# Gate columns of the delta rule as TensorE's weights, and its output in two groups of matmuls

## What is computed

```python
beta = jax.nn.sigmoid(dn_b)                       # dn_b, dn_a: 4 + 4 columns of the projection h @ w_in
g = -jnp.exp(dn_A_log) * jax.nn.softplus(dn_a + dn_dt_bias)

def step(state, inp):                             # over 4 chunks of 64 tokens, for 4 heads
    u_c, w_c, a_c, qd_c, kt_c, dl_c = inp
    v_new = u_c - jnp.einsum('bhck,bhkv->bhcv', w_c, state)
    o = jnp.einsum('bhck,bhkv->bhcv', qd_c, state) + jnp.einsum('bhcj,bhjv->bhcv', a_c, v_new)
    state = state * dl_c[..., None, None] + jnp.einsum('bhck,bhcv->bhkv', kt_c, v_new)
    return state, o
```

## Time and profile before

| | |
|---|---|
| median of 3 runs | 1917.99 us (1915.57 to 1919.57) |
| the profiled execution's own time | 1917.77 us |
| its span | 1916.0 us |
| mean granted clock of TensorE | 0.993 |
| TensorE matmul, busy | 1888.3 us (99%), 14788 records |
| VectorE, busy | 1252.2 us (65%) |
| ScalarE, busy | 956.3 us (50%) |
| GpSimd, busy | 308.2 us (16%) |

### The profile page before, as it was taken

The page is one execution under the profiler, slowest core; times in us unless marked ns, Lnnn a source line. Parts: engine busy times, 40 slices in busy tenths (PEclk is TensorE's granted clock), DMA queues, the critical chain, the costliest instruction groups (busy, mean ns, idle before and its releaser), DMA issues.

```text
span 1916.0 us, 35058 instructions
## 1 busy us (share of the span) xinstructions
PE 1888.3 (99%) x14788; PEld 1806.2 (94%) x14788; DVE 1252.2 (65%) x1678; ACT 956.3 (50%) x1381; POOL 308.2 (16%) x176
## 2 busy tenths in 40 slices
PE   7999999999999999999999999999999999999998
PEld 7999998998899999999989999999999899999998
DVE  6884567665689545777648775576647694567643
ACT  5634456444563345564445445555534445556533
POOL 0050221000003103200001352320001352221000
PEclk9999999999999999999999999999999999999999
DMA  6443344666545323555565553456655663445553
GB/s 227 160 143 111 112 154 153 205 195 209 163 135 165 111 99 122 201 173 190 193 195 176 183 187 122 133 181 190 191 187 171 218 193 115 136 169 187 186 188 100
DMA packets 92156, 317.50 MB, mean 166 GB/s; under 512 B 11744, under 2 KB 12896, under 8 KB 91744
## 3 DMA queue, kind: packets, MB, share of 16 engines
q1 hardware_dynamic: 91424, 314.69, 50.2%
q10 hardware_dynamic: 576, 0.57, 0.1%
HBM read 304.99 MB, written 1.05 MB: 160 GB/s over the span
## 4 chain that ended last, share of the span: by engine, by line
PE 84%; DVE 11%; ACT 2%; DMA 1%; issue 1%; SPq 0%; DVEq 0%; ACTq 0%
PE bank L2001 82%; DVE wlo L1126 4%; DVE area L1126 3%; DVE area L1132 1%; DMA raw<-in_weights 1%; ACT area L630 1%; PE bank L2512 1%; DVE hl L1132 1%; DVE xT L1132 1%; ACT whi L636 1%; PE bank L2220 1%; DVE area L1645 1%; DVE area L1643 0%; PE bank L2530 0%; ACT L618 0%
## 5 line engine op out<-in xcount | busy, mean ns | idle before, releaser
L1126 DVE TENSOR_TENSOR wlo<-raw,whi 128x1024 fp32r<-128x1024 f32 x518 | 666.3, 1301 | 402.6 <-ACT whi L636 402.2
L2001 PE MATMUL bank<-hh,whi 128*128 128x256 f32 x2928 | 834.5, 286 | 15.1 <-DVE wlo L1126 11.7
L2001 PE MATMUL bank<-hh,wlo 128*128 128x256 f32 x2928 | 818.2, 280 | 0.0
L2001 PE MATMUL bank<-hl,whi 128*128 128x256 f32 x2928 | 811.3, 280 | 0.0
L636 ACT CAST whi<-raw 128x1024 fp32r<-128x1024 f32 x572 | 589.4, 1046 | 415.7 <-PE bank L2001 369.9
L2001 PEld LDWEIGHTS bank<-hh,whi 128*128 128x128 f32 x2928 | 555.7, 190 | 28.4 <-DVE wlo L1126 15.1
L2001 PEld LDWEIGHTS bank<-hl,whi 128*128 128x128 f32 x2928 | 555.2, 191 | 1.9 <-issue 1.9
L2001 PEld LDWEIGHTS bank<-hh,wlo 128*128 128x128 f32 x2928 | 556.0, 190 | 0.0
L1781 POOL TENSOR_TENSOR area<-area 128x512 f32<-128x512 f32 (+4 forms) x86 | 136.7, 1596 | 567.8 <-DVE area L1132 249.8
L1781 POOL TENSOR_TENSOR wlo<-raw,whi 128x1024 fp32r<-128x1024 f32 x54 | 134.3, 2488 | 427.9 <-ACT whi L636 427.9
L2001 PE MATMUL bank<-area 128*128 128x128 f32 (+5 forms) x1544 | 199.9, 288 | 1.2 <-DVE area L1196 0.7
(11 more groups left out here) (127 smaller groups left out, 1918.3 us busy)
## 6 DMA issues: line engine op xcount, KB each, us to landing
raw<-in_weights SPq DMA_DIRECT2D x572, 512.0 KB, 4.1
area<-area SPq DMA_DIRECT2D x96, 64.0 KB, 3.6
area<-area SPq DMA_DIRECT2D x16, 128.0 KB, 4.0
cst<-in_const SPq DMA_DIRECT2D x1, 1188.0 KB, 8.3
cst<-in_const SPq DMA_DIRECT2D x1, 1024.5 KB, 6.9
xT<-in_x SPq DMA_DIRECT2D x4, 256.0 KB, 8.1
out<-xT SPq DMA_DIRECT2D x4, 256.0 KB, 2.9
area<-in_lev SPq DMA_DIRECT2D x2, 384.0 KB, 6.6
```

The source lines that it names most:

```text
L1126: return v.tensor_tensor(dst, x, y, op)
L2001: return e.matmul(ps, x, y, start=start, stop=stop, skip_group_check=skip)
```

## The change

The gate columns: SW becomes TensorE's weights (16 or 8 columns) and the 256 tokens move, in 16 matmuls which stand before chunk 4. They give a tile of 16 rows (8 of the high part and the small products, 8 of the low part) by 256 tokens. DVE copies it to `ABR` in SBUF inside the hook. After chunk 4 two matmuls with a constant of two stacked 8 x 8 unit matrices, sent along with `small`, transpose it and add the two parts, and DVE multiplies by RST straight from the bank. ACT's cast to SW and DVE's subtraction move one step ahead. The output: for n > 0 first four matmuls with the state's weights, then four with VN, and only the first matmul into each bank sets the start flag.

```diff
-N_SMALL = 64 + 512
+N_SMALL = 64 + 512 + 8
...
+        ABR = SM[0:16, 0:256]
...
                 def hook():
                     factor(norm)
-                    a.wait_ge(s_small[L], 16)
-                    a.copy(SW[:, :, 0:8], sm3).then_inc(*a_dn.up("SW", L))
...
                 next(qkv)
                 next(qkv)
+                a.wait_ge(s_small[L], 16)
+                a.copy(SW[:, :, 0:8], sm3).then_inc(*a_dn.up("SW", L))
                 next(qkv)
                 next(qkv)
                 a.wait_ge(*v_dn.at("ab", L))
...
                 def hook():
                     factor(norm)
-                    v.wait_ge(*a_dn.at("SW", L))
-                    tt(SW[:, :, 8:16], sm3, SW[:, :, 0:8].bitcast(F32), OP.subtract).then_inc(*v_dn.up("SW", L))
+                    v.wait_ge(*e_dn.at("abrow", L))
+                    v.tensor_copy(ABR, bank[1][0:16, 0:256]).then_inc(*v_dn.up("abrow", L))
...
                 next(qkv)
                 next(qkv)
+                v.wait_ge(*a_dn.at("SW", L))
+                tt(SW[:, :, 8:16], sm3, SW[:, :, 0:8].bitcast(F32), OP.subtract).then_inc(*v_dn.up("SW", L))
                 next(qkv)
                 next(qkv)
-                two = bank[1][:, 0:32].rearrange("p (s c) -> p s c", s=2)
                 v.wait_ge(*e_dn.at("ab", L))
-                v.tensor_copy(tmp2, two[:, :, 8:16]).then_inc(*v_dn.up())
-                v.wait_ge(*v_dn.now())
-                tt(AB2, two[:, :, 0:8], tmp2, OP.add).then_inc(*v_dn.up("absum", L))
-                v.wait_ge(*v_dn.now())
                 v.wait_ge(*v_norm.at("turned", norm))
-                tt(AB2, AB2, wide(RST[:, :], 2, 8), OP.mult).then_inc(*v_dn.up("ab", L))
+                tt(AB2, bank[1][:, 256:272].rearrange("p (s c) -> p s c", s=2), wide(RST[:, :], 2, 8), OP.mult).then_inc(*v_dn.up("ab", L))
...
+                    def place(h):
+                        return bank[2 + h // 2][:, 256 * (h % 2) + 64 * n:256 * (h % 2) + 64 * n + 64]
+
+                    if n:
+                        for h in range(4):
+                            mm(place(h), St[:, 128 * h:128 * h + 128], Aq[:, 256 * h + 64 * n:256 * h + 64 * n + 64], h % 2 == 0, False, True)
                     for h in range(4):
                         b = 2 * h + half
-                        o = bank[2 + h // 2][:, 256 * (h % 2) + 64 * n:256 * (h % 2) + 64 * n + 64]
-                        if n:
-                            mm(o, St[:, 128 * h:128 * h + 128], Aq[:, 256 * h + 64 * n:256 * h + 64 * n + 64], True, False)
-                        x = mm(o, hv(VN)[r, h, :], AT[r, 128 * b + 64 * q:128 * b + 64 * q + 64], n == 0, True)
+                        x = mm(place(h), hv(VN)[r, h, :], AT[r, 128 * b + 64 * q:128 * b + 64 * q + 64], n == 0, True, True)
...
                 next(qkv)
                 next(qkv)
                 next(qkv)
+                e.wait_ge(*v_dn.at("SW", L))
+                fresh(1, v_dn.at("ab", L))
+                for k in range(8):
+                    mm(bank[1][0:16, 0:T], SW[:, k, :], hh[:, k, :], k == 0, False, True)
+                    x = mm(bank[1][0:8, 0:T], SW[:, k, 0:8], hl[:, k, :], False, k == 7, True)
+                x.then_inc(*e_dn.up("abrow", L))
                 next(qkv)
-                e.wait_ge(*v_dn.at("SW", L))
-                fresh(1, v_dn.at("absum", L))
+                e.wait_ge(*v_dn.at("abrow", L))
                 for s in range(2):
-                    for k in range(8):
-                        mm(bank[1][:, 16 * s:16 * s + 16], hh[:, k, 128 * s:128 * s + 128], SW[:, k, :], k == 0, False, True)
-                        x = mm(bank[1][:, 16 * s:16 * s + 8], hl[:, k, 128 * s:128 * s + 128], SW[:, k, 0:8], False, k == 7, True)
+                    x = mm(bank[1][:, T + 8 * s:T + 8 * s + 8], ABR[:, 128 * s:128 * s + 128], small[0:16, 576:584], True, True)
                 x.then_inc(*e_dn.up("ab", L))
...
+        small[l][0:16, 576:584] = np.tile(np.eye(8, dtype=np.float32), (2, 1))
```

More of the change, by code:

```diff
@@ L398, in program @@
         u1, u2 = SM[:, 128:136], SM[:, 144:152]
-        AB2, tmp2 = (SM[:, c:c + 16].rearrange("p (s c) -> p s c", s=2) for c in (192, 224))
+        AB2 = SM[:, 192:208].rearrange("p (s c) -> p s c", s=2)
         AB = SM[:, 192:208].rearrange("p (s c) -> p c s", s=2)
+        ABR = SM[0:16, 0:256]
         sm3 = small[:, 0:64].rearrange("p (k c) -> p k c", c=8)
```

## The result

| | before | after |
|---|---|---|
| median | 1915.57 us (1910.08 to 1919.57, 5 runs) | 1926.87 us (1925.66 to 1929.29, 5 runs) |
| ratio | | 1.0064, 95% interval 1.0047 to 1.0081 |
| span of the profiled execution | 1916.0 us | 1925.1 us |

A forecast was written before the change was run, and what follows sets the result against it. The prediction took TensorE (PE), busy 99% of the span, to bound the kernel. Gate columns 3.0, output 5.3 and clock 3.4 us sum to 11.7 us off 1917.8, so 1906.1 us, range 1900.5 to 1912.5.

The forecast's parts named there:

- rival 5: DVE stands in the hook for the 16 new matmuls: time level at 0.47 us each, 1932.5 at half clock; chance 0.03.
- The gate columns, 3.0 us: Cheaper gate-column matmuls; chunk 13 gains only what DVE's row gains: 1.0 us in layer 0, 2.0 in layer 1.
- Rival 1: Gate columns give all of PE's saving, 2 x 4.3 us, DVE's row being tighter or ACT earlier: 1900.5 us; chance 0.08.
- the sign of being wrong that the prediction names: Chunk 13 starting much sooner than 55.4 (layer 0) or 553.1 less layer 0's gains (layer 1) would show the forecast wrong.
- The output, 5.3 us: Delta rule's output: grouping four St, then four VN saves array-shape changes, 0.89 us in each of six groups.
- rival 4: Grouping the delta rule's output saves only the VN half, about 0.5 us each, 3 us: 1908.3 us; chance 0.05.
- the upper bound of a group: Delta rule's output: at most 1.05 us saved per group (6.3 in all), if St costs what VN does.
- The clock, 3.4 us: After the output groups of layers 0 and 1, both falls of the clock to half vanish, saving 3.4 us.
- rival 3: The clock has nothing to do with the change, all four falls stay: 7.1 us off, 1910.7 us; chance 0.08.
- Rival 2: The clock still falls twice after the outputs, or at other places: 3.4 us less saved, 1909.4 us; chance 0.17.
- The sum, 11.7 us: Whole kernel: 3.0 + 5.3 + 3.4 us off 1917.8 us, giving 1906.1; chance 0.57 for its own range 1904 to 1909.

The follow-up runs named there:

- experiment 1: The kernel before with only 8 unused columns added behind `small`, moving every tile behind it 32 bytes: 1941.22 us, ratio 1.0157.
- 3: The kernel before with only the delta rule's output grouped, all addresses as before: 1905.64 us, ratio 0.9951.
- 8: The kernel before with 16 more columns of `small`, everything behind it 64 bytes further on: 1948.54 us, ratio 1.0179.
- 4: The changed kernel's gate columns alone, output in pairs as before, tiles 64 bytes higher: 1946.83 us, ratio 1.0185 to the kernel before.
- experiment 9: The changed kernel with hh, hl, RSB, SW and the area 128 bytes behind their old place: 1919.68 us, ratio 1.0035 to the kernel before.
- experiment 5: The changed kernel with RST moved behind the area, so hh, hl, RSB, SW and the area keep their old addresses: 1902.85 us, ratio 0.9919 to the kernel before.
- 6: The changed kernel with hh, hl and RSB 32 bytes on, the area at its old place: 1916.15 us, ratio 1.0012 to the kernel before.
- 7: The changed kernel with the area 32 bytes on, hh, hl, RSB and SW at their old places: 1905.23 us, ratio 0.9962 to the kernel before.
- 12: The changed kernel with hh, hl, RSB, SW and the area 256 bytes behind their old place: 1904.74 us, ratio 0.9944 to the kernel before.

## Why the prediction was wrong

**The step that failed is one that was never made.** The sum costs what the diff removes, adds and moves among the instructions. Its first line, `N_SMALL = 64 + 512 + 8`, stands in no term: the place of the tiles behind it was put at nothing, without a reason. It moves the operands of nearly every matmul by 32 bytes, and that costs 29 us (experiment 1), two and a half times everything forecast. The prediction also took 0.11 to 0.12 us as *the* distance of a 256-column matmul and never asked why it varies by 4% within one trace, from 113 to 118 ns. No rival has it either: rival 5, the one on the slower side, was DVE standing in the hook for the 16 matmuls, and these took 1.98 us in all.

**What bounds the kernel** was right, and it is why the move costs so much: PE is busy 99% of the span, so 27.3 us more of matmul time make 29 us.

**The gate columns, 3.0 us.** Right within 0.4 us in this pair of traces: from the norm's sum to chunk 13 layer 0 gained 1.2 us (forecast 1.0), and in layer 1 the kernel went from 2.40 us behind to 0.25, 2.15 (forecast 2.0). The other traces bear it out. Where the gate columns are new, from the norm's sum to chunk 13 is 30.8 us in both layers of all ten. Where they are old, it is 32.05 and 32.98 (before), 32.69 and 31.98 (experiment 1), 30.93 and 31.39 (3), 32.96 and 32.31 (8). That is 3.4, 3.1, 0.7 and 3.7 us for both layers together, 2.7 on average, and the least where the clock fell for the shortest time. Rival 1 is refuted by it. What is missing to its 4.3 us per layer is, as argued, lost to waits for wlo such as the one before chunk 13, 0.38 us before 53.95. Chunk 13 at 53.95 instead of 55.4 looked like the sign of being wrong that the prediction names; nearly all of it is the 1.3 us of the start.

**The output, 5.3 us.** The group of n = 2 is 0.84 us shorter, 0.89 was forecast, and rival 4 with its 0.5 us is refuted by that. The runs give 6.6 us at the old place and 9.9 at 64 bytes for the term and its share of the clock (forecast: 5.3 and up to 3.4, so 8.7). Two slips of the working carry no weight: 0.84 is 58% of 1.45 us and not half, and the upper bound of a group is 1.03 us and not 1.05.

**The clock, 3.4 us.** Right in kind: experiments 3 and 4 each remove the falls of one place. By the records of the clock in all fourteen traces, it fell at the old gate columns in both layers of all four traces that have them, and at the new ones in none of twenty cases. It fell in or within a microsecond behind 12 of 24 output groups in pairs, and behind 2 of 60 grouped ones (the one at 681.4 us in the changed kernel and one in experiment 9). So rival 3, that the clock has nothing to do with the change, is refuted, and with it the reading that only idle gaps of PE matter: PE was busy throughout in all those stretches. Rival 2 was half right: where the clock falls and for how long, 3.4 or 6.8 us, changes from one trace to the next, and one fall is left in the changed kernel. The Trainium skill (TensorE: Matmul & The Clock Gate, "HAM oscillation") warns of gaps in which PE is idle, but does not say that nothing else makes the clock fall. The prediction read that into it, and the falls here are a case that the section does not cover.

**The sum, 11.7 us.** At a fixed place it was of the right size: 14.35 us at 32 bytes, 11.6 at 64, and 10.8 by the medians at the old place (0.81% by the ratio, which is 15.5 us, with an interval of 0.48% to 1.14%). The first two are differences of times from different comparisons, in which the kernel before had other medians; by the ratios to it they are 0.9% and 0.4%, 18 and 8.5 us. So the size is known to within several us only, and these times can't tell rivals 1 and 4 from the forecast, as the rows above do. The forecast of 1906.1 us is thus the time of a kernel that was not the one changed: experiment 5 took 1902.85. That it came so near is in part luck, for the kernel before took 1912 to 1916 us in the comparisons and not the 1917.8 that the sum starts from.

## What to carry to other kernels

Read a diff for what it moves in memory as well as for what it moves in time: a table that grows, a new tile or another order of allocation shifts every operand behind it, and in a kernel bound by TensorE, as this one is, that can outweigh the change. Before a change is judged, print the addresses of both versions and hold those of the matmuls' operands fixed, or time the old kernel at the new addresses too; one look at the distance of matmuls in code that the diff does not touch tells whether this is needed. And where a mean distance is made of two kinds of stretches, the cause of the second kind is worth a question before the sum is made.

## What was not expected of the hardware

- The distance of 256-column fp32r matmuls depends on the place of the moving tile in SBUF, tried in steps of 32 bytes and more: 115.1, 118.3, 119.9, 116.8, 117.4, 118.7 and 116.2 ns on average at 0, 32, 64, 96, 128, 192 and 256 bytes from an address of 88000 (hh), 96192 (hl) and 105920 (area). The place of the weights' tile counts too: in the 512-column matmuls whi or wlo moves, which stayed where they were, and the distance goes with the place of hh and hl or of the area, from which the weights come (229.2 ns and 233.3 in experiments 6 and 7). They have another order, 227.0 ns at 64 bytes, where the 256-column ones are slowest, and 233.3 at 32, 96 and 128.
- At the old place one and the same code has two rates. Layer 0 and layer 1 run the same program, and a stretch of 72 matmuls took 8.58 us in the one and 8.89 in the other (rows below), with distances near 113 ns from the fifth matmul on in layer 0 and near 118 ns in layer 1. With it goes the spread of the runs: the kernel before ranged from 1897.91 to 1922.23 us over the comparisons, the changed kernel over 4 us and its version at 64 bytes over 2. The profiled executions of experiments 5 and 12, the same instructions with means of 115.1 and 116.2 ns, are 13.7 us apart, of which the 1.1 ns on 11,400 distances are 12.5 (an estimate). What chooses the rate is open.
- The slow start of 0.213 us per 256-column matmul, of which the trace has no record of the clock, and whose end moves between 12.1 and 18.8 us from one execution to the next. In the pair of traces above, 4.4 us more of it went with 1.3 us of time.
- The clock falls to half behind matmuls with few moving columns, though PE never idles. With denser matmuls in the same place (16 of 256 columns for 32 of 16 and 8; groups of 3.15 us for 4.0 us) nearly all falls were gone: none of 20 and 2 of 60, for 8 of 8 and 12 of 24.
- Not settled: why a place is slow; whether it is hh's own address that counts or its distance from whi and wlo, which stayed where they were; whether hh and hl count apart; which accesses of other engines or of the DMA take part. None of this was tried.

The two rates of one program, timeline of PE in the kernel before, layer 0 and layer 1:

```profile
65.24 0.68 PE L2001 MATMUL bank<-hh,whi 128*128 128x256 f32 x1
...
73.82 0.59 PE L2001 MATMUL bank<-area,cst 128*128 128x512 f32 x1
...
563.68 0.68 PE L2001 MATMUL bank<-hh,whi 128*128 128x256 f32 x1
...
572.57 0.59 PE L2001 MATMUL bank<-area,cst 128*128 128x512 f32 x1
```
